# Two half groups of conditioning products summed on VectorE, and the last conditioning products of two groups moved into the norm passages

## The chip, the cores and the metric

The kernel runs on one core of one Trainium2 chip. The number that counts is the device time of one execution in microseconds (us); before the change it is 1595.04 us, the median of 3 runs from 1594.56 to 1595.25 us. The engines are named PE (TensorE, matrix products), DVE (VectorE), ACT (ScalarE), POOL (GpSimd) and SP (the engine that issues the weight loads).

## What is computed

The reference is a transformer of two blocks on 256 tokens of width 1024 (and 256 context tokens in the first layer). What the change touches is the conditioning of the first block:

```python
silu_c, silu_cc = jax.nn.silu(c), jax.nn.silu(c_ctx)
for i in range(2):
    sh1, sc1, g1, sh2, sc2, g2 = split(silu_c @ ada_w[i] + ada_b[i], 6)
    csh1, csc1, cg1, csh2, csc2, cg2 = split(silu_cc @ ada_w[i] + ada_b[i], 6)
    h = rmsnorm(x, norm_mix[i]) * (1.0 + sc1) + sh1      # and hc with csc1, csh1
    x = x + g1 * attention(h, hc)
    h2 = rmsnorm(x, norm_ffn[i]) * (1.0 + sc2) + sh2
    x = x + g2 * conv_ffn(h2)
```

`ada_w[i]` has 1024 rows and 6144 columns. Two vectors (`silu_c`, `silu_cc`) are multiplied with it in layer 0; in layer 1 the context needs only the first third.

## The kernel before

All weights come through one stream, `wstream`, in units of 128 x 2048 numbers (1 MB). `unit_orders` writes the order of the units (`KEYS`) and the order in which PE uses them (`RUNS`). SP loads unit v into buffer v % 3 of `RAW`, and `load_unit` first waits until unit v - 3 has been used up. An ordinary unit is used up when ACT has copied it to its rounded high part (`split_hi`, L526) and DVE or POOL has subtracted to get the low part (`split_lo`, L536), both in `WHL`, which also has three buffers. PE then makes three products for each pair of tiles (L554, L555, L556). Units are split two or three ahead of their use on PE, and every engine takes its instructions strictly in the order in which they are written.

A conditioning unit, key `("ada", b, k)`, is not split. `pe_ada` multiplies it as it stands: `CB` (128 rows, 32 columns, the two vectors in columns 0 and 1) is the stationary operand, the raw unit the moving one, in four products that write the four strips of 32 partitions of one PSUM bank, `AB`. Group b has eight units (four for b = 5 and 6). When a group is complete, ACT copies the bank to `TMP` (`act_ada_row`), PE turns it (`pe_ada_turn`, L599) and DVE adds the bias (`dve_ada`).

Group 1 is spread over the first QKV phase: two units behind each of `("qkv", 0, 3)`, 4 and 5, one behind 6 and 7. Group 3 has two units in the second norm passage, two ahead of up unit 0, and one ahead of each of the up units 2 to 5. Group 4 is made already in another way: DVE multiplies each unit by one vector's column and adds it to `WSUM` (`dve_ada_step`), and `pe_ada_joint` closes the sum over partitions with a column of ones (L586). Of group 5, units 0 to 2 stand in the norm passage ahead of layer 1, and unit 3 behind the first QKV unit; of group 6, units 0 to 2 stand in the norm passage ahead of up unit 0 of layer 1, and unit 3 behind that unit.

In the QKV phase of layer 0, `dve_qkv` does for each unit u: low part of unit u + 3, then the rotation of the two heads of unit u (`stream_shuffle`, a product with the sine table L1106, a sum L1109); the rotation needs a cosine product of POOL (L1121), and POOL makes half of the low parts of every second unit and of all from unit 8.

Of the kernel before, what the change touches and what calls it, by code (L numbers as in the profile page):

```python
# [6 lines left out]
F32 = mybir.dt.float32  # L7
# [142 lines left out]
def unit_orders():  # L150
# [15 lines left out]
    late_ada = iter(range(DT))  # L166
    for i in range(8):
        add(("qkv", 0, i), 1 if i < 3 else 2)
        for _ in range((0, 0, 0, 2, 2, 2, 1, 1)[i]):
            k = next(late_ada)  # L170
            add_ada(1, k)
            run_ada(1, k)
    for i in range(4):
        add(("qkv", 0, 8 + i), 1)
# [8 lines left out]
    for j in range(HALF_FT):  # L183
        add(("up", 0, j), 2)
        for k in {1: range(4), 2: (4,), 3: (5,), 4: (6,), 5: (7,)}.get(j, ()):
            add_ada(3, k)
# [16 lines left out]
    for j in range(FT):  # L203
        add(("up", 1, j), 1000)
        for k in {0: (0, 1, 2), 1: (3,)}.get(j, ()):
            add_ada(6, k)
# [21 lines left out]
    for name, at, b in (("up", UP_ADA, 3), ("qkv", QKV_ADA, 5), ("up", LATE_ADA, 6), ("up", JOINT_ADA, 4)):  # L228
        for key, ks in at.items():
            r = runs.index(key)  # L230
            runs[r:r] = [("ada", b, k) for k in ks]
    return keys, every, runs
# [63 lines left out]


# [67 lines left out]
def bass_two_block_decoder(nc, wstream, first, small, consts, late, rpb, xin, out):  # L365
    ctx = ExitStack()
    with ctx:
# [102 lines left out]
        c_silu, c_zero, lam_v, lam_exp = (sem(n) for n in ("c_silu", "c_zero", "lam_v", "lam_exp"))  # L470
# [88 lines left out]
        def pe_ada(e, b, k):  # L559
            v = UNIT_OF["ada", b, k]  # L560
            if k == 0 and b == 1:
                e.wait_ge(f_par, DT)
            elif k == 0:
                e.wait_ge(ada_par, b - 1)
            e.wait_ge(d_raw[v % 3], 16 * (v // 3 + 1))
            for j in range(4):
                c = k if b < 5 else 2 * k + j // 2
                mm = e.matmul(AB[32 * j:32 * j + 32, :], CB[:, c, :], RAW[:, v % 3, 512 * j:512 * j + 512],  # L568
                              start=k == 0, stop=k == ada_units(b) - 1)
            mm.then_inc(gemm, 1)  # L570

        def dve_ada_step(e, k):
            v = UNIT_OF["ada", 4, k]
            e.wait_ge(d_raw[v % 3], 16 * (v // 3 + 1))
            if k == 0:
                e.tensor_scalar(WSUM[:, :], RAW[:, v % 3, :], CB[:, k, 0:1], None, ALU.mult).then_inc(ada_acc, 1)
                return
            e.wait_ge(ada_acc, k)
            e.scalar_tensor_tensor(out=WSUM[:, :], in0=RAW[:, v % 3, :], scalar=CB[:, k, 0:1], in1=WSUM[:, :],
                                   op0=ALU.mult, op1=ALU.add).then_inc(ada_acc, 1)  # L580
# [469 lines left out]
        def act_qkv(e, l):  # L1050
            for u, i in enumerate(QKV_ORDER[l]):
# [24 lines left out]
                if l == 0 and i == 7:  # L1076
                    act_ada_row(e, 1)
# [3 lines left out]
            for i in range(4):  # L1081
# [402 lines left out]
        def pe_wo(e, l):  # L1484
            T, n = (512, 1) if l == 0 else (256, 3)
            for i in range(4):
# [32 lines left out]
            pe_ada(e, 6 if l else 3, 1)  # L1519
# [69 lines left out]
        def pe_ffn(e, l):  # L1589
            T, ring = (512, 3) if l == 0 else (256, 6)  # L1590
            for c, js in chunks(l):
                for jj, j in enumerate(js):
# [1438 lines left out]
        def act_start(e):  # L3031
# [3 lines left out]
            e.wait_ge(c_zero, 5)  # L3035
# [12 lines left out]
        def dve_start(e):  # L3048
# [6 lines left out]
            e.memset(CB[:, :, :], 0.0).then_inc(c_zero, 1)  # L3055
# [24 lines left out]
        def pool_start(e):  # L3080
            pool_rsqrt(e, 0)
# [288 lines left out]
```

## Time and profile before

| | |
|---|---|
| Median of 3 runs | 1595.04 us |
| The profiled execution | 1595.22 us |
| Its span, first to last instruction | 1593.4 us |
| Mean granted clock of TensorE | 0.997 |
| PE busy | 1568.6 us (98%) |
| DVE busy | 936.4 us (59%) |
| ACT busy | 750.5 us (47%) |
| POOL busy | 543.3 us (34%) |
| Share of PE in the chain that ended last | 88% |

Times in the rows are counted from the start of the span. The busy time of PE is the union of its matmuls, whose ends overlap the start of the next; how long a group of products really takes is therefore read from the starts around it.

### The profile page before, as it was taken

Reading aid. Unit: us, or ns where it says so; the run is one execution under the profiler, and the core shown is the slowest. Engines: PE = TensorE matmul, PEld = TensorE weight load, DVE = VectorE, ACT = ScalarE, POOL = GpSimd, SP = SyncE. Lnnn points to the kernel's source line nnn. Section 1 sums busy time; section 2 is a strip of 40 time slices with the busy share of each in tenths; the row PEclk is TensorE's granted clock in tenths of the full one; section 3 lists DMA queues with packets and bytes.
Section 4 is the critical chain, followed back from the end, with each engine's and each line's share of the span. In section 5 each row is a group of like instructions: output and inputs, shape, how many; then the busy total and the mean of one; then the engine's idle time right before and its main releaser. Section 6 shows DMA issues by size and latency. Waiting matters only on the chain.

```text
span 1593.4 us, 23097 instructions
## 1 busy us (share of the span) xinstructions
PE 1568.6 (98%) x9146; PEld 1303.4 (82%) x9146; DVE 936.4 (59%) x1441; ACT 750.5 (47%) x1360; POOL 543.3 (34%) x354
## 2 busy tenths in 40 slices
PE   8999999999999999999999999999999999999998
PEld 5778557778887888879768899989998889998887
DVE  4434485555575554342266888757876457968435
ACT  5324485444322433243375755445654445654444
POOL 2224243322211222212273111007424657623663
PEclk9999999999999999999999999999999999999999
DMA  9264500534174222364313754454534534633551
GB/s 393 94 246 187 212 30 9 204 135 157 63 268 184 80 81 73 124 207 164 123 37 113 267 192 172 162 190 170 183 133 161 199 143 171 215 133 132 185 211 54
DMA packets 52603, 249.17 MB, mean 156 GB/s; under 512 B 20624, under 2 KB 21008, under 8 KB 26256
## 3 DMA queue, kind: packets, MB, share of 16 engines
q1 hardware_dynamic: 43744, 243.90, 42.2%
q10 hardware_dynamic: 8752, 3.80, 1.0%
q8 instruction: 73, 1.20, 0.3%
q14 instruction: 34, 0.28, 0.0%
HBM read 246.63 MB, written 1.05 MB: 155 GB/s over the span
## 4 chain that ended last, share of the span: by engine, by line
PE 88%; DVE 5%; ACT 3%; issue 1%; DMA 1%; POOL 1%; SPq 0%; POOLq 0%; ACTq 0%; DVEq 0%
PE psq L554 16%; PE psq L555 16%; PE psq L556 16%; PE ps L554 7%; PE ps L556 7%; PE ps L555 7%; PE psq L970 3%; PE ps L568 1%; PE psq L971 1%; PE ps L970 1%; DMA RAW<-wstream 1%; ACT WHL L526 1%; PE psq L1365 1%; PE ps L1393 1%; PE psq L2298 1%
## 5 line engine op out<-in xcount | busy, mean ns | idle before, releaser
L536 DVE TENSOR_TENSOR WHL<-RAW,WHL 128x1024 fp32r<-128x1024 f32 (+3 forms) x264 | 324.9, 1254 | 290.1 <-ACT WHL L526 289.6
L536 POOL TENSOR_TENSOR WHL<-RAW,WHL 128x1024 fp32r<-128x1024 f32 (+2 forms) x116 | 304.5, 2627 | 504.6 <-ACT WHL L526 471.8
L526 ACT ACTIVATE WHL<-RAW 128x1024 fp32r<-128x1024 f32 (+2 forms) x380 | 361.4, 1002 | 196.1 <-DMA RAW<-wstream 98.6
L554 PE MATMUL psq<-NHL,WHL 128*128 128x256 f32 (+1 forms) x1072 | 353.8, 330 | 1.7 <-POOL WHL L536 0.7
L555 PE MATMUL psq<-NHL,WHL 128*128 128x256 f32 (+1 forms) x1072 | 349.0, 326 | 0.0
L556 PE MATMUL psq<-NHL,WHL 128*128 128x256 f32 (+1 forms) x1072 | 348.9, 325 | 0.0
L554 PEld LDWEIGHTS psq<-NHL,WHL 128*128 128x128 f32 x1072 | 205.2, 191 | 28.9 <-issue 7.5
L556 PEld LDWEIGHTS psq<-NHL,WHL 128*128 128x128 f32 x1072 | 205.3, 191 | 16.6
L555 PEld LDWEIGHTS psq<-NHL,WHL 128*128 128x128 f32 x1072 | 205.3, 191 | 15.4
L554 PE MATMUL psq<-WHL,NHL 128*128 128x512 f32 (+1 forms) x320 | 124.8, 390 | 1.7 <-DVE WHL L536 1.7
L556 PE MATMUL psq<-WHL,NHL 128*128 128x512 f32 (+1 forms) x320 | 123.3, 385 | 0.0
L555 PE MATMUL psq<-WHL,NHL 128*128 128x512 f32 (+1 forms) x320 | 123.2, 385 | 0.0
L554 PE MATMUL ps<-NHL,WHL 128*128 128x512 f32 (+1 forms) x272 | 94.9, 349 | 0.0
L555 PE MATMUL ps<-NHL,WHL 128*128 128x512 f32 (+1 forms) x272 | 94.1, 346 | 0.0
L556 PE MATMUL ps<-NHL,WHL 128*128 128x512 f32 (+1 forms) x272 | 94.0, 346 | 0.0
L1716 DVE SCALAR_TENSOR_TENSOR TMP<-psq,SMALL,TMP 128x510 f32<-128x510 f32 (+1 forms) x64 | 39.2, 613 | 79.7 <-ACT TMP L1677 79.7
L699 ACT ACTIVATE TMP<-X 128x256 f32<-128x256 f32 (+1 forms) x52 | 25.1, 498 | 120.7 <-DVE X L1532 59.9
L1677 ACT ACTIVATE TMP<-psq,SMALL 128x512 f32<-128x512 f32 (+1 forms) x64 | 40.8, 666 | 87.0 <-PE psq L556 87.0
L554 PEld LDWEIGHTS psq<-WHL,NHL 128*128 128x128 f32 x320 | 60.1, 188 | 14.3 <-DVE WHL L536 2.1
L556 PEld LDWEIGHTS psq<-WHL,NHL 128*128 128x128 f32 x320 | 60.1, 188 | 11.5
L555 PEld LDWEIGHTS psq<-WHL,NHL 128*128 128x128 f32 x320 | 60.1, 188 | 11.0
L1752 POOL TENSOR_TENSOR HL<-TMP,HH 128x512 fp32r<-128x512 f32 x22 | 28.8, 1308 | 112.9 <-ACT HH L1663 112.9
(389 smaller groups left out, 2975.6 us busy)
## 6 DMA issues: line engine op xcount, KB each, us to landing
RAW<-wstream SPq DMA_DIRECT2D x194, 1024.0 KB, 4.8
RAW<-wstream SPq DMA_DIRECT2D x32, 704.0 KB, 4.0
K<-first SPq DMA_DIRECT2D x4, 1024.0 KB, 17.2
RAW<-wstream SPq DMA_DIRECT2D x4, 800.0 KB, 4.3
X<-xin SPq DMA_DIRECT2D x2, 1024.0 KB, 6.1
V<-first SPq DMA_DIRECT2D x2, 1024.0 KB, 19.3
Q<-first SPq DMA_DIRECT2D x2, 1024.0 KB, 24.7
BR<-rpb ACTq DMA_DIRECT2D x8, 256.0 KB, 8.2
```

The lines of the kernel that those rows point to most:

```text
L526: e.activation(WH[:, u % 3, a:z], RAW[:, v % 3, a:z], ACT.Copy).then_inc(w_hi, 1)
L536: e.tensor_tensor(WL[:, u % 3, a:z], RAW[:, v % 3, a:z], WH[:, u % 3, a:z].bitcast(F32), ALU.subtract).then_inc(w_lo_p if pool else w_lo_v, 1)
L554: e.matmul(o, lh, rh, start=start, stop=False)
L555: e.matmul(o, lh, rl, start=False, stop=False)
L556: return e.matmul(o, ll, rh, start=False, stop=stop)
L568: mm = e.matmul(AB[32 * j:32 * j + 32, :], CB[:, c, :], RAW[:, v % 3, 512 * j:512 * j + 512], start=k == 0, stop=k == ada_units(b) - 1)
L699: e.activation(sq_tile(n, m), X[:, m, 0:NORM_T[n]], ACT.Square).then_inc(x_sq, 1)
L970: e.matmul(o[:, 0:512], wh, x, start=start, stop=False, skip_group_check=True)
L971: return e.matmul(o[:, 0:256], wl, x[:, 0, :], start=False, stop=stop, skip_group_check=True)
L1677: e.activation(acc_tile(l, U, s), up_banks(l, jj)[s][:, :], ACT.Identity, scale=small_at("fconv", (3 * l + 1) * 44 + j + FT * s), bias=sma ...
L1716: e.scalar_tensor_tensor(out=a3[:, :, 1:256], in0=o3[:, :, 0:255], scalar=w(0), in1=a3[:, :, 1:256], op0=ALU.mult, op1=ALU.add).then_inc(u ...
L1752: e.tensor_tensor(HL[l][:, jj, :], acc_tile(l, U, 0), HH[l][:, jj, :].bitcast(F32), ALU.subtract).then_inc(h_lo, 1)
```

## The change

Group 1: units 0, 1, 6 and 7 are multiplied by both vectors and summed on DVE, units 2 to 5 stay on PE in two pairs, and a joint product of the two sums stands behind `("qkv", 0, 8)`. Group 3: units 0 to 3 stay on PE, 4 to 7 are summed on DVE beside the up units 1, 3, 5 and 7, and the joint stands ahead of up unit 8. The sums of group 1 lie in parts of `PP` and `TMP`, those of group 3 in `WSUM`, which is now twice as long. The column of ones is a column of `CB`, and POOL clears `CB` instead of DVE. The fourth unit of the groups 5 and 6 goes into the norm passage ahead of them. The order of the stream follows.

```diff
-UP_ADA = {("up", 0, 0): (0, 1, 2, 3), ("up", 0, 2): (4,), ("up", 0, 3): (5,), ("up", 0, 4): (6,), ("up", 0, 5): (7,)}
-QKV_ADA = {("qkv", 1, 4): (0, 1, 2), ("qkv", 1, 5): (3,)}
-JOINT_ADA = {("up", 0, HALF_FT + 1): (7,)}
-LATE_ADA = {("up", 1, 0): (0, 1, 2), ("up", 1, 1): (3,)}
+FIRST_ADA = {3: (0,), 4: (1,), 5: (2, 3), 6: (4, 5), 9: (6,), 10: (7,)}
+FIRST_SUMMED = {1: (0,), 2: (1,)}
+FIRST_ON_PE = {5: (2, 3), 6: (4, 5)}
+UP_SUMMED = {1: 4, 3: 5, 5: 6, 7: 7}
+QKV_ADA = {("qkv", 1, 4): (0, 1, 2, 3)}
+LATE_ADA = {("up", 1, 0): (0, 1, 2, 3)}
+SUMMED = {1: (0, 1, 6, 7), 3: (4, 5, 6, 7), 4: tuple(range(8))}
+JOINT_AT = {("qkv", 0, 9): 1, ("up", 0, 8): 3, ("up", 0, HALF_FT + 1): 4}
...
         def load_unit(e, v):
...
-            if v >= 3 and KEYS[v - 3][:2] == ("ada", 4):
-                e.wait_ge(ada_acc, KEYS[v - 3][2] + 1)
+            if v >= 3 and KEYS[v - 3] in ADA_ACC:
+                e.wait_ge(ada_acc, ADA_ACC[KEYS[v - 3]])
...
+        def weight_sums(b):
+            if b == 1:
+                return [t.rearrange("p a n -> p (a n)") for t in (PP[:, 3:7, :], TMP[:, 4:8, :])]
+            return [WSUM[:, c, :] for c in range(1 if b == 4 else 2)]
+
+        def dve_ada_step(e, b, k):
+            v = UNIT_OF["ada", b, k]
+            sums = weight_sums(b)
+            at = ADA_ACC["ada", b, k] - len(sums)
             e.wait_ge(d_raw[v % 3], 16 * (v // 3 + 1))
+            if b == 4 and k == 0:
+                e.wait_ge(gemm, product(("joint", 3)))
+            for c, t in enumerate(sums):
+                if k == SUMMED[b][0]:
+                    e.tensor_scalar(t, RAW[:, v % 3, :], CB[:, k, c:c + 1], None, ALU.mult).then_inc(ada_acc, 1)
+                    continue
+                e.wait_ge(ada_acc, at - len(sums) + c + 1)
+                e.scalar_tensor_tensor(out=t, in0=RAW[:, v % 3, :], scalar=CB[:, k, c:c + 1], in1=t,
+                                       op0=ALU.mult, op1=ALU.add).then_inc(ada_acc, 1)
...
+        def pe_ada_joint(e, b):
+            if b == 4:
+                e.wait_ge(ada_par, 3)
+            e.wait_ge(ada_acc, ADA_ACC["ada", b, SUMMED[b][-1]])
+            for c, t in enumerate(weight_sums(b)):
+                for j in range(4):
+                    mm = e.matmul(AB[32 * j:32 * j + 32, :], ONE_AT[c], t[:, 512 * j:512 * j + 512], start=b == 4,
+                                  stop=b == 4 or c == 1)
             mm.then_inc(gemm, 1)
...
             for i in range(4):
                 if l == 0 and i == 1:
+                    pe_ada_joint(e, 1)
+                if l == 0 and i == 2:
                     pe_ada_turn(e, 1)
                 pe_values(e, l, i)
...
         def dve_qkv(e, l):
             for u, i in enumerate(QKV_ORDER[l]):
+                if l == 0:
+                    for k in FIRST_SUMMED.get(i, ()):
+                        dve_ada_step(e, 1, k)
                 split_lo(e, ahead(("qkv", l, i)), False)
...
-            dve_ada(e, 1 if l == 0 else 5)
+            if l == 0:
+                dve_ada_step(e, 1, 6)
+                dve_ada_step(e, 1, 7)
             for i in range(3):
+                if i == (1 if l == 0 else 0):
+                    dve_ada(e, 1 if l == 0 else 5)
                 split_lo(e, ahead(("qkv", l, 8 + i)), False)
...
                 if (l, i) == (1, 3):
                     pe_ada(e, 6, 0)
+                    pe_ada(e, 6, 1)
...
-            pe_ada(e, 6 if l else 3, 1)
+            pe_ada(e, 6 if l else 3, 2 if l else 1)
...
+                        if jj == 8:
+                            pe_ada_joint(e, 3)
...
-                    if l == 1 and j < 2:
-                        pe_ada(e, 6, 2 + j)
+                    if l == 1 and j == 0:
+                        pe_ada(e, 6, 3)
...
+                    if l == 0 and j in UP_SUMMED:
+                        dve_ada_step(e, 3, UP_SUMMED[j])
                     split_lo(e, ahead(key), False)
```

The first place is DVE at the end of the QKV phase of layer 0. WHL is the low part, the K rows are the rotation of the last QKV unit, and ADA is the bias sum that closes group 1. Before:

```order
L536 TENSOR_TENSOR WHL<-RAW,WHL 128x1024
L1104 STREAM_SHUFFLE TMP<-TMP 128x256
L1106 TENSOR_TENSOR TMP<-TMP,CONST 128x256
L1109 TENSOR_TENSOR K<-K,TMP 128x256
L1104 STREAM_SHUFFLE TMP<-TMP 128x256
L1106 TENSOR_TENSOR TMP<-TMP,CONST 128x256
L1109 TENSOR_TENSOR K<-K,TMP 128x256
L619 TENSOR_TENSOR ADA<-ps,SMALL 128x32
L536 TENSOR_TENSOR WHL<-RAW,WHL 128x1024 x3
```

The same place now, where L549 is the low part, L1142 the end of a head's rotation, and L602 a step of the sums:

```order
L549 TENSOR_TENSOR WHL<-RAW,WHL 128x1024
L1137 STREAM_SHUFFLE TMP<-TMP 128x256
L1139 TENSOR_TENSOR TMP<-TMP,CONST 128x256
L1142 TENSOR_TENSOR K<-K,TMP 128x256
L1137 STREAM_SHUFFLE TMP<-TMP 128x256
L1139 TENSOR_TENSOR TMP<-TMP,CONST 128x256
L1142 TENSOR_TENSOR K<-K,TMP 128x256
L602 SCALAR_TENSOR_TENSOR PP<-RAW,CB,PP 128x2048
L602 SCALAR_TENSOR_TENSOR TMP<-RAW,CB,TMP 128x2048
L602 SCALAR_TENSOR_TENSOR PP<-RAW,CB,PP 128x2048
L602 SCALAR_TENSOR_TENSOR TMP<-RAW,CB,TMP 128x2048
L549 TENSOR_TENSOR WHL<-RAW,WHL 128x1024
```

Four steps over 2048 columns stand between the last rotation and the next low part. The second place is PE between `("qkv", 0, 8)` and `("qkv", 0, 9)`. Before, only the turn of group 1 (L599) stands there:

```order
L554 MATMUL psq<-WHL,NHL 128x512
L555 MATMUL psq<-WHL,NHL 128x512
L556 MATMUL psq<-WHL,NHL 128x512
L599 MATMUL ps<-CONST,TMP 128x128 x4
L554 MATMUL psq<-WHL,NHL 128x512
L555 MATMUL psq<-WHL,NHL 128x512
```

Now the joint of group 1 (L614) stands there, and the turn comes one unit later:

```order
L567 MATMUL psq<-WHL,NHL 128x512
L568 MATMUL psq<-WHL,NHL 128x512
L569 MATMUL psq<-WHL,NHL 128x512
L614 MATMUL ps<-PP,CB 32x512 x4
L614 MATMUL ps<-TMP,CB 32x512 x4
L567 MATMUL psq<-WHL,NHL 128x512
L568 MATMUL psq<-WHL,NHL 128x512
```

The joint waits for the last of the four steps on DVE. The third place is PE in the norm passage ahead of layer 1 (L737 sums of squares, L808 the row of scales, L568 conditioning products, L918 and L920 the first QKV unit). Before:

```order
L737 MATMUL ps<-ONES,TMP 128x64 x4
L568 MATMUL ps<-RAW,CB 32x512 x4
L808 MATMUL ps<-CONST,RS 128x128 x4
L568 MATMUL ps<-RAW,CB 32x512 x4
L918 MATMUL psq<-NHL,WHL 128x512
L920 MATMUL psq<-NHL,WHL 128x512
```

And now, with L765, L836, L581, L946 and L948 for the same things:

```order
L765 MATMUL ps<-ONES,TMP 128x64 x4
L581 MATMUL ps<-RAW,CB 32x512 x4
L836 MATMUL ps<-CONST,RS 128x128 x4
L581 MATMUL ps<-RAW,CB 32x512 x8
L946 MATMUL psq<-NHL,WHL 128x512
L948 MATMUL psq<-NHL,WHL 128x512
```

Two conditioning units in place of one stand ahead of the first QKV product.

## Rows read from the trace of the kernel before

**Rows 1.** The page, part 1: PE's busy time, share and instructions.

```profile
PE 1568.6 (98%) x9146; PEld 1303.4 (82%) x9146; DVE 936.4 (59%) x1441; ACT 750.5 (47%) x1360; POOL 543.3 (34%) x354
```

**Rows 2.** Timeline of PE around two units: start, duration, line, shapes.

```profile
75.41 0.39 PE L556 MATMUL psq<-NHL,WHL 128*128 128x512 f32 x1
...
77.93 0.40 PE L555 MATMUL psq<-NHL,WHL 128*128 128x512 f32 x1
...
88.41 0.39 PE L556 MATMUL psq<-NHL,WHL 128*128 128x512 f32 x1
```

**Rows 3.** Timeline of PE around the last single unit of group 1.

```profile
126.52 0.39 PE L556 MATMUL psq<-NHL,WHL 128*128 128x512 f32 x1
...
128.17 0.39 PE L555 MATMUL psq<-WHL,NHL 128*128 128x512 f32 x1
```

**Rows 4.** Instructions on WSUM: count, ns min/median/max, first and last start.

```profile
L579 DVE SCALAR_TENSOR_TENSOR WSUM<-RAW,CB,WSUM x7: 2345/2349/3192, 440.2 to 482.4; 128x2048 f32<-128x2048 f32 x7
L576 DVE TENSOR_SCALAR WSUM<-RAW,CB x1: 1279/1279/1279, 438.9 to 438.9; 128x2048 f32<-128x2048 f32 x1
```

**Rows 5.** Loads into RAW issued between 113 and 117 us, and their landing.

```profile
L511 SPq DMA_DIRECT2D RAW<-wstream x2: 328/352/377, 115.9 to 116.3; - x2
...
DMA to landing us min/median/max: 4.7/5.8/6.8
```

**Rows 6.** Timeline of ACT: the high part of the eighth QKV unit.

```profile
120.57 2.01 ACT L526 ACTIVATE WHL<-RAW 128x1024 fp32r<-128x1024 f32 x2 [7.06 <-DMA RAW<-wstream]
```

**Rows 7.** Timeline of DVE at the end of the QKV phase, layer 0.

```profile
121.67 1.23 DVE L536 TENSOR_TENSOR WHL<-RAW,WHL 128x1024 fp32r<-128x1024 f32 x1 [4.90 <-ACT WHL L526]
...
131.66 0.43 DVE L1104 STREAM_SHUFFLE TMP<-TMP 128x256 f32<-128x256 f32 x1
...
134.22 1.22 DVE L536 TENSOR_TENSOR WHL<-RAW,WHL 128x1024 fp32r<-128x1024 f32 x1
...
135.84 2.13 DVE L1106 TENSOR_TENSOR TMP<-TMP,CONST 128x256 f32<-128x256 f32 x1
...
140.21 0.43 DVE L1109 TENSOR_TENSOR K<-K,TMP 128x256 f32<-128x256 f32 x1
```

**Rows 8.** Timeline of POOL: its halves of two low parts there.

```profile
122.66 2.51 POOL L536 TENSOR_TENSOR WHL<-RAW,WHL 128x1024 fp32r<-128x1024 f32 x1 [7.46 <-ACT WHL L526]
...
134.89 2.80 POOL L536 TENSOR_TENSOR WHL<-RAW,WHL 128x1024 fp32r<-128x1024 f32 x1 [4.25 <-ACT WHL L526]
```

**Rows 9.** Timeline of PE's weight loads near the start.

```profile
3.32 0.34 PEld L742 LDWEIGHTS psq<-PP 128*128 128x128 f32 x1 [0.52 <-issue]
...
10.68 0.30 PEld L742 LDWEIGHTS psq<-PP 128*128 128x128 f32 x2 [0.84 <-issue]
```

**Rows 10.** A stretch: us, then busy PE, PEld, DVE, ACT, POOL; granted clock.

```profile
320.00:420.00 100.00, 100.00 (x455) 79.06 (x454) 57.17 (x61) 43.97 (x59) 24.58 (x15) 1.00 0.37 137
```

**Rows 11.** Timeline of PE in the norm passage ahead of layer 1.

```profile
686.42 1.06 PE L568 MATMUL ps<-RAW,CB 128*32 128x512 f32 x8
688.17 0.47 PE L918 MATMUL psq<-NHL,WHL 128*128 128x512 f32 x1 [0.69 <-ACT NHL L851]
```

**Rows 12.** The load of the group's fourth unit, and its landing.

```profile
L511 SPq DMA_DIRECT2D RAW<-wstream x1: 327/327/327, 683.0 to 683.0; - x1
...
DMA to landing us min/median/max: 4.8/4.8/4.8
```

**Rows 13.** Timeline of PE in the norm passage of layer 1.

```profile
875.78 1.06 PE L568 MATMUL ps<-RAW,CB 128*32 128x512 f32 x8
877.67 1.55 PE L737 MATMUL ps<-ONES,TMP 128*128 128x64 f32 x12 [0.82 <-POOL TMP L719]
...
882.26 0.36 PE L918 MATMUL psq<-NHL,WHL 128*128 128x256 f32 x1 [0.29 <-ACT NHL L851]
```

**Rows 14.** Two loads issued between 874 and 878 us, and their landing.

```profile
L511 SPq DMA_DIRECT2D RAW<-wstream x2: 327/328/328, 874.6 to 876.9; - x2
...
DMA to landing us min/median/max: 4.8/5.0/5.1
```

More of the change, by code:

```diff
@@ L164, in run_ada @@
         runs.append(("ada", b, k))
[L166 to L170, printed above, removed]
+    for i in range(12):
+        add(("qkv", 0, i), 1 if i < 3 or i >= 8 else 2)
+        for k in FIRST_ADA.get(i, ()):
             add_ada(1, k)
+        for k in FIRST_ON_PE.get(i, ()):
             run_ada(1, k)
-    for i in range(4):
-        add(("qkv", 0, 8 + i), 1)
     for i in range(2):
@@ L184, in unit_orders @@
         add(("up", 0, j), 2)
-        for k in {1: range(4), 2: (4,), 3: (5,), 4: (6,), 5: (7,)}.get(j, ()):
+        for k in {1: range(4), 2: (4,), 4: (5,), 6: (6,), 8: (7,)}.get(j, ()):
             add_ada(3, k)
@@ L204, in unit_orders @@
         add(("up", 1, j), 1000)
-        for k in {0: (0, 1, 2), 1: (3,)}.get(j, ()):
+        for k in {0: (0, 1, 2, 3)}.get(j, ()):
             add_ada(6, k)
@@ L227, in unit_orders @@
             add(("out", l, i), 1)
-    for name, at, b in (("up", UP_ADA, 3), ("qkv", QKV_ADA, 5), ("up", LATE_ADA, 6), ("up", JOINT_ADA, 4)):
+    for at, b in ((UP_ADA, 3), (QKV_ADA, 5), (LATE_ADA, 6)):
         for key, ks in at.items():
@@ L231, in unit_orders @@
             runs[r:r] = [("ada", b, k) for k in ks]
+    for key, b in JOINT_AT.items():
+        r = runs.index(key)
+        runs[r:r] = [("joint", b)]
     return keys, every, runs
@@ L295, in product_end @@
     return GEMM_BEFORE[KEYS[v]] + unit_products(KEYS[v])
+ADA_ACC = {}
+acc_count = 0
+for b_, ks_ in SUMMED.items():
+    for k_ in ks_:
+        acc_count += 1 if b_ == 4 else 2
+        ADA_ACC["ada", b_, k_] = acc_count
 SPLIT_UNITS = [v for v, k_ in enumerate(KEYS) if k_[0] != "ada"]
@@ L560, in pe_ada @@
             v = UNIT_OF["ada", b, k]
-            if k == 0 and b == 1:
+            if b == 1 and k == 2:
                 e.wait_ge(f_par, DT)
@@ L568, in pe_ada @@
                 mm = e.matmul(AB[32 * j:32 * j + 32, :], CB[:, c, :], RAW[:, v % 3, 512 * j:512 * j + 512],
-                              start=k == 0, stop=k == ada_units(b) - 1)
+                              start=k == (2 if b == 1 else 0), stop=k == ada_units(b) - 1)
             mm.then_inc(gemm, 1)
-        def dve_ada_step(e, k):
-            v = UNIT_OF["ada", 4, k]
-            e.wait_ge(d_raw[v % 3], 16 * (v // 3 + 1))
[L575 to L580, printed above, removed]
@@ L588, in pe_ada_joint @@
             mm.then_inc(gemm, 1)
         def act_ada_row(e, b):
-            e.wait_ge(gemm, product(("ada", b, ada_units(b) - 1)))
+            e.wait_ge(gemm, product(("joint", b) if b in SUMMED else ("ada", b, ada_units(b) - 1)))
             if b >= 2:
@@ L1000, in pe_qkv @@
             n = 2 * l
-            late_ada = iter(range(DT))
             for u, i in enumerate(QKV_ORDER[l]):
@@ L1022, in pe_qkv @@
                 if l == 0:
-                    for _ in range((0, 0, 0, 2, 2, 2, 1, 1)[i]):
-                        pe_ada(e, 1, next(late_ada))
+                    for k in FIRST_ON_PE.get(i, ()):
+                        pe_ada(e, 1, k)
             for i in range(4):
                 if l == 0 and i == 1:
+                    pe_ada_joint(e, 1)
+                if l == 0 and i == 2:
                     pe_ada_turn(e, 1)
@@ L1599, in pe_ffn @@
                     if l == 0 and c == 0:
-                        for k in UP_ADA.get(("up", 0, jj), ()):
-                            if k > 1:
-                                pe_ada(e, 3, k)
+                        if jj == 0:
+                            pe_ada(e, 3, 2)
+                            pe_ada(e, 3, 3)
+                        if jj == 8:
+                            pe_ada_joint(e, 3)
                         if jj == 9:
```

29 lines of the change are left out of this document (15 added, 14 removed).

## The prediction

> **What bounds the kernel now.** I read the page's engine shares first. The reader is to see that PE is busy for 1568.6 of 1593.4 us and DVE for 936.4 [rows 1]: PE is the bound, and a microsecond taken from PE or added to it in a dense stretch moves the end by as much. Then the timeline of PE, for what one conditioning group really takes; then the DVE, ACT, POOL and load rows around 120 to 141 us, since the change makes PE wait there for DVE; last the two norm passages.
>
> In a QKV unit a product of 512 columns follows the one before at (88.41 - 77.93) / 46 = 0.228 us [rows 2]. With a pair of conditioning units between, L555 comes 2.52 us after the last L556, where two steps would be 0.46: a pair costs 2.06 us [rows 2]. A single unit costs 128.17 - 126.52 - 0.46 = 1.19 us [rows 3].
>
> **Group 1, the products.** Before: three pairs and two singles, 3 x 2.06 + 2 x 1.19 = 8.56 us. Now two pairs and the joint, which has the shape and count of a pair: 6.18. That is **-2.4 us** on PE.
>
> **Group 1, the new wait.** The joint waits for DVE's steps 6 and 7. When does PE arrive? At 128.17 it starts the second product of QKV unit 8 with 8.56 us of groups behind it; now only two pairs, 4.12, are behind it, so it is there at 123.73, and 47 more steps of 0.228 bring it to the joint at 134.4.
>
> When is DVE done? The load of QKV unit 8 is issued behind a conditioning product: at 115.9, landing after 4.7 [rows 5], and ACT starts on it at 120.57 [rows 6]. In the new order it waits for the first product of the pair behind QKV unit 6, which comes two pairs (4.1 us) earlier; so ACT starts at 116.5 and DVE's low part at 117.6 in place of 121.67 [rows 7]. From 121.67 to the last sum of the rotation at 140.21 + 0.43 = 140.64 DVE works almost without a gap [rows 7], so the change's earlier loads bring it forward by 4.1 us, to 136.5. The load of QKV unit 10 is no longer late: its buffer comes free with POOL's half, at 122.66 + 2.51 - 4.1 = 121.1 [rows 8], so it lands at 125.9 and POOL's half of it (2.80 us [rows 8]) starts near 128. POOL's work then lies beside the rotation of unit 6 in place of that of unit 7. A rotation of two heads takes 134.22 - 131.66 = 2.6 us alone, and 5.2 (140.64 less 135.44) with POOL's half beside it, one table product of 2.13 us among it [rows 7]; it hits one or the other, so the end stays about 136.5. Behind it come four steps of 2.35 us [rows 4], 9.4 in all: step 7 ends at 145.9. Queued behind them are the low part of QKV unit 11, which PE needs two units later, and the bias sum, which now waits for a later turn; neither holds anybody.
>
> So PE waits 145.9 - 134.4 = 11.5 us. Bounds: if POOL disturbed nothing, the low part of unit 10 is done one half high part and 1.2 us after 125.9, near 128.1, the rotation at 130.7 and the steps at 140.1: 5.7 us. With all four steps at the slowest row, 3.19 us [rows 4], it is 14.9. I take **+11.0 us**, near the sum from the rows, since the disturbed rotation is what the trace shows. There is nothing behind the joint that PE could do first; its queue is in order. ACT takes the row out of the bank behind the joint, and the turn comes a unit later, hidden.
>
> **The clock after the wait.** No stretch of the trace shows a wait of PE this long in the middle; the granted clock is 1.00 in the up phase [rows 10]. At the start of the span, after PE had done nothing, a weight load of 128 columns takes 0.34 us at 3.32 and 0.15 at 10.68 (two in 0.30) [rows 9]: the lower of its two levels, 1.2 GHz, and then the upper, 2.4. The level rose somewhere between, so 3.3 to 10.7 us at the low level would lose half of that, 1.6 to 5.3 us. Whether 11 us of waiting brings it down, the rows can't say; below it is nothing. I take **+2.0 us**, near the smaller price.
> The Trainium skill, "TensorE: Matmul & The Clock Gate", Part 1 (The HAM clock gate), says that an idle PE falls back to half rate and gets the full rate back only after working for a while. By that rule the term is certain and not only likely; the start of this trace agrees with the second half of it, and the first is not shown. Without the rule the sum would be 2 us lower.
>
> **Group 3.** Four singles (4.76 us) become one joint pair (2.06): **-2.7 us**. DVE gets 2 x 1.28 + 6 x 2.35 = 16.7 us more [rows 4] over eight up units. It is busy 57 of 100 us there while PE has no gap [rows 10], a unit is split two ahead and PE's next use of a bank is three units off, so a step of 4.7 us in every second unit is covered by 43 us of idle DVE. If that cover failed, one late step would cost up to 4.7. Step 7 ends in the middle of up unit 7, before the joint. The joint of group 4 is as it was.
>
> **The norm passages.** Each loses a single group behind the first unit, -1.19. In the passage ahead of layer 1 the third product starts at 686.42 and ends by 687.4; the load of the fourth unit was issued at 683.0 and lands after 4.8, at 687.8 [rows 12]; the fourth product then runs to 688.9, where the first QKV product starts now at 688.17 after a wait of 0.69 for ACT [rows 11]. So +0.7 and -1.2: **-0.5**. In layer 1 the second product goes into the 0.82 us that PE waits for POOL before the sums at 877.67 [rows 13], 875.78 + 2 = 877.8, no loss. The third and fourth units are the loads of 874.6 and 876.9, landing after 4.8 to 5.1 [rows 14], the last at 881.9; its product ends at 882.9, against 882.26 for the first up product now [rows 13]. Again +0.7 - 1.2: **-0.5**. Bounds for the two together: -2.4, if nothing were late, to +1.0, if the scales came late as well.
>
> **The rest.** CB cleared by POOL instead of DVE: the first products at the start wait for the sums of squares and for loads, not for it; 0. Loads of group 1 that now wait for DVE's steps 0 and 1 (2.6 and 4.7 us, some 10 us ahead of PE's need): 0.
>
> **Sum.** -2.4 + 11.0 + 2.0 - 2.7 - 0.5 - 0.5 = +6.9. Against the profiled execution's own 1595.22 us (span 1593.4 and 1.8 around it) this is 1602.1; that execution lies 0.2 above the median of the runs, so I say 1602 us. All that the change removes, 6.1 us, is less than the one wait that it makes.
>
> **Rivals.**
> 1. *DVE is nearly in time (the faster side).* If the joint waits less than 3 us and the clock stays, the time is 1589.1 (no wait) to 1592. For it: DVE is busy only 59% overall [rows 1]. Against: four steps of 2.35 us can't start before the rotation of unit 7, whose last input PE delivers itself only 11 us before it arrives at the joint, and 9.4 us of these are the steps. It decides where wait and clock together fall below 6.1 us. Chance 0.11.
> 2. *A shorter wait, warm.* The wait is 5.7 to 9 us, as POOL disturbs less, and the clock holds: 1595 to 1598. For it: the lower bound above. Chance 0.16.
> 3. *The clock comes back late.* The price of the clock is 5.3 instead of 2.0, or the wait 14: 1605 to 1608. Chance 0.08.
> 4. *DVE is late in the up phase too.* One step of 4.7 us uncovered: 1607. Against it the 43% of idle DVE [rows 10]. Chance 0.03.
> The forecast (wait 9 to 13, clock 0 to 3) has 0.62, and its own range is 1598 to 1605.
>
> **Chances and range.** This kernel can be told from no change by about 0.2%, 3.2 us. The forecast but for a sliver (0.03), rivals 3 and 4 and a small part of the second (0.03) are slower by more: 0.73. Within 0.2% are the most of the second and that sliver: 0.16. Faster: the first rival, 0.11. The range 1595.5 to 1606 leaves out the first rival and the far end of the third.
>
> **What would show it.** Right: in the profile after, PE has one gap of about 11 us before the joint of group 1 near 134 us, released by DVE's step on TMP, and the steps are four of 2.35 us in a row behind the rotation; weight loads just behind it at 0.34 us if the clock fell; no gap at the joint of group 3; the first products behind the two passages 0.7 us later and the group behind the first unit gone. Wrong: the last step of group 1 ends before PE is done with QKV unit 8, or the loads of that phase come later than I have them, so that PE waits elsewhere first.

## The result, and the profile after

The changed kernel takes 1603.43 us (median of 4 runs, 1603.0 to 1604.47) against 1595.04 us before: a ratio of 1.0054, 95% interval 1.0037 to 1.0071. It is slower by 8.4 us, where 1602 was predicted. Its profiled execution took 1603.0 us, with a span of 1601.2 against 1593.4.

First the line of the page that answers to [rows 1]:

```profile
PE 1564.5 (98%) x9114; PEld 1302.8 (81%) x9114; DVE 969.8 (61%) x1456; ACT 749.3 (47%) x1360; POOL 542.4 (34%) x356
```

PE is busy 4.1 us less, and the span is 7.8 us longer. So what is new is mostly time in which PE does nothing. The waits of PE (whole span; engine, operand and line, what released it: us in total, times, longest) name it at the top of the list:

```profile
PE ps L614 <- DVE TMP L602: 11.1, 1, 11.1
...
PE psq L567 <- DVE WHL L549: 2.4, 3, 0.8
PE ps L581 <- DMA RAW<-wstream: 2.3, 4, 1.1
```

L614 is the joint's product, L602 the step of a weighted sum on VectorE. The timeline of PE at the joint of group 1, and behind it the first products of QKV unit 9:

```profile
146.54 1.93 PE L614 MATMUL ps<-PP,CB 128*32 128x512 f32 x8 [11.12 <-DVE TMP L602]
148.25 1.93 PE L614 MATMUL ps<-TMP,CB 128*32 128x512 f32 x8
150.11 0.80 PE L567 MATMUL psq<-WHL,NHL 128*128 128x512 f32 x1
150.70 0.63 PE L568 MATMUL psq<-WHL,NHL 128*128 128x512 f32 x1
151.13 0.46 PE L569 MATMUL psq<-WHL,NHL 128*128 128x512 f32 x1
151.43 0.40 PE L567 MATMUL psq<-WHL,NHL 128*128 128x512 f32 x1
```

One gap of 11.12 us. Then the joint takes 150.11 - 146.54 = 3.57 us, and a QKV product 0.6 to 0.8 us in place of 0.4: the clock fell. The granted clock by stretches (columns as in [rows 10]; the granted clock is the number behind POOL's) shows the two levels, 2.4 GHz as 1.00 and 1.2 GHz as 0.50:

```profile
118.50:146.50 28.00, 16.92 (x75) 13.48 (x73) 26.58 (x31) 8.35 (x18) 11.94 (x9) 0.84 0.45 166
...
130.00:135.00 5.00, 5.00 (x23) 4.14 (x23) 4.90 (x9) 0.00 (x0) 2.95 (x3) 1.00 0.49 192
135.00:138.00 3.00, 0.42 (x2) 0.00 (x0) 2.86 (x8) 0.00 (x0) 0.00 (x0) 0.93 0.00 0
138.00:150.50 12.50, 3.96 (x17) 0.98 (x18) 9.71 (x5) 2.26 (x3) 1.35 (x1) 0.50 0.59 223
151.00:152.00 1.00, 1.00 (x5) 0.77 (x5) 0.00 (x0) 0.00 (x0) 0.60 (x1) 0.87 0.36 139
```

The reader is to see VectorE in them as well: busy for 26.58 of the 28 us up to the joint (the first row), and for 2.86 of 3 where PE begins to idle. It is no idle engine that PE waits for. Its timeline, with the three slow table products of the rotations, the last sum of the rotation, and the first and the last of the four steps:

```profile
120.62 1.80 DVE L1139 TENSOR_TENSOR TMP<-TMP,CONST 128x256 f32<-128x256 f32 x1
...
124.20 2.15 DVE L1139 TENSOR_TENSOR TMP<-TMP,CONST 128x256 f32<-128x256 f32 x1
...
129.12 2.56 DVE L1139 TENSOR_TENSOR TMP<-TMP,CONST 128x256 f32<-128x256 f32 x1
...
137.01 0.42 DVE L1142 TENSOR_TENSOR K<-K,TMP 128x256 f32<-128x256 f32 x1
137.35 2.34 DVE L602 SCALAR_TENSOR_TENSOR PP<-RAW,CB,PP 128x2048 f32<-128x2048 f32 x1
...
144.14 2.34 DVE L602 SCALAR_TENSOR_TENSOR TMP<-RAW,CB,TMP 128x2048 f32<-128x2048 f32 x1
```

How far the changed kernel stands behind the one before, by the same row of PE in both traces (starts in us; the last column is a second profiled execution of the changed kernel, out of the experiments):

| place | before | changed | difference | changed, second execution |
|---|---|---|---|---|
| last selection product of the start | 55.24 | 55.92 | +0.68 | -0.06 |
| first unit of group 2, behind the gap | 177.18 | 189.09 | +11.91 | +11.34 |
| joint of group 4, behind group 3 | 507.82 | 516.85 | +9.03 | +8.59 |
| first unit of group 5 (passage ahead of layer 1) | 681.88 | 690.92 | +9.04 | +8.59 |
| turn of group 5 | 750.74 | 758.76 | +8.02 | +7.60 |
| first unit of group 6 (passage in layer 1) | 875.78 | 883.80 | +8.02 | +7.61 |
| turn of group 6 | 918.69 | 926.85 | +8.16 | +7.79 |
| span | 1593.4 | 1601.2 | +7.8 | +7.8 |

### The profile page after: what moved, and what is told of

It is laid out like the page before. It is cut to its first block, busy times and chain, and to the rows that moved or that the text cites. A ratio compares the mean times of both kernels' runs of the same rounds, so it can differ in the third digit from the quotient of the medians.

```text
span 1601.2 us, 23057 instructions
## 1 busy us (share of the span) xinstructions
PE 1564.5 (98%) x9114; PEld 1302.8 (81%) x9114; DVE 969.8 (61%) x1456; ACT 749.3 (47%) x1360; POOL 542.4 (34%) x356
## 4 chain that ended last, share of the span: by engine, by line
PE 81%; DVE 10%; ACT 4%; issue 2%; DMA 2%; POOL 1%; ACTq 0%; POOLq 0%; SPq 0%; DVEq 0%
PE psq L567 14%; PE psq L569 14%; PE psq L568 14%; PE ps L567 7%; PE ps L569 7%; PE ps L568 7%; PE psq L998 3%; DVE WHL L549 2%; ACT WHL L539 2%; PE psq L999 1%; PE ps L998 1%; DMA RAW<-wstream 1%; PE psq L1402 1%; PE ps L1430 1%; PE ps L1417 1%
## 5 line engine op out<-in xcount | busy, mean ns | idle before, releaser
L549 DVE TENSOR_TENSOR WHL<-RAW,WHL 128x1024 fp32r<-128x1024 f32 (+3 forms) x264 | 329.6, 1272 | 257.8 <-ACT WHL L539 257.3
L549 POOL TENSOR_TENSOR WHL<-RAW,WHL 128x1024 fp32r<-128x1024 f32 (+2 forms) x116 | 302.5, 2610 | 496.5 <-ACT WHL L539 463.8
L568 PE MATMUL psq<-NHL,WHL 128*128 128x256 f32 (+1 forms) x1072 | 348.2, 325 | 0.0
L568 PEld LDWEIGHTS psq<-NHL,WHL 128*128 128x128 f32 x1072 | 204.6, 191 | 15.6
L568 PE MATMUL psq<-WHL,NHL 128*128 128x512 f32 (+1 forms) x320 | 123.4, 386 | 0.0
L568 PE MATMUL ps<-NHL,WHL 128*128 128x512 f32 (+1 forms) x272 | 94.1, 346 | 0.0
L568 PEld LDWEIGHTS psq<-WHL,NHL 128*128 128x128 f32 x320 | 60.3, 188 | 11.0
```

What stands on the lines that cost most here:

```text
L549: e.tensor_tensor(WL[:, u % 3, a:z], RAW[:, v % 3, a:z], WH[:, u % 3, a:z].bitcast(F32), ALU.subtract).then_inc(w_lo_p if pool else w_lo_v, 1)
L568: e.matmul(o, lh, rl, start=False, stop=False)
```

## The experiments

Eight kernels were run, in two batches; all but the repeat are edits of the changed kernel. An edit is shown as the lines that say it; comments stand for the rest. Ratios are against the kernel before, run beside them on the same chip (medians 1595.62 and 1595.13 us), with the 95% interval.

### The joint one unit and a quarter later

```
-JOINT_AT = {("qkv", 0, 9): 1, ...
+JOINT_AT = {("qkv", 0, 10): 1, ...
 # pe_values, per quarter t of a unit
+    if l == 0 and i == 2 and t == 1:
+        pe_ada_joint(e, 1)
+    if l == 0 and i == 2 and t == 2:
+        pe_ada_turn(e, 1)
 # act_qkv: act_ada_row(e, 1) between the evictions t = 1 and t = 2 of unit 9
```

> The joint of group 1 stands one unit of V and a quarter later (behind the first quarter of unit 10, its turn behind the second, the copy of its row in the midst of the evictions of V's first half); nothing else differs from the changed kernel. PE would then come to the joint at about 135.4 + 10.5 + 2.6 = 148.5 us, 2 us after the last step (146.5). Theory A (the wait of 11.1 us is all that is wrong, and the slow clock behind it is its consequence): no wait at the joint, no granted clock of 0.50 from 138 to 151, attention and all behind it earlier by 11.1 + 2.3 = 13.4 us: 1603.4 - 13.4 = 1590.0, under the kernel before. Theory B (PE at the joint only waits in place of something later: the split of unit 11, whose load also hangs on the steps and whose high part ran at 147.1 in the changed kernel): some of it comes back as a wait for unit 11's low part or at the first scores, 1593 to 1600. Theory C (the clock falls here whether or not PE waits): 1592.3.

Measured: 1589.93 us (5 runs, 1589.46 to 1592.26), ratio 0.9965 (0.9952 to 0.9979). PE's joint has no wait in the timeline, and the stretch in which PE idled is full at a granted clock of 1.00:

```profile
148.31 1.06 PE L614 MATMUL ps<-PP,CB 128*32 128x512 f32 x8
149.19 1.04 PE L614 MATMUL ps<-TMP,CB 128*32 128x512 f32 x8
```

```profile
138.00:142.00 4.00, 4.00 (x19) 3.32 (x18) 4.00 (x3) 0.00 (x0) 0.00 (x0) 1.00 0.02 6
142.00:147.00 5.00, 5.00 (x24) 4.14 (x23) 4.34 (x2) 0.28 (x1) 0.00 (x0) 1.00 0.81 305
```

VectorE does the same steps at the same time (the first at 137.21, the last until 146.35 us); only PE's order differs. The first unit of group 2 starts at 175.06, 2.12 us ahead of the kernel before. Theory A holds and B falls: nothing else was waiting behind the joint. C falls too, by the clock of 1.00. This kernel is faster than the changed one by 13.5 us and faster than the one before by 0.35%.

### The joint directly ahead of unit 10

The edit is against the late joint:

```
-    if l == 0 and i == 2 and t == 1:
+    if l == 0 and i == 2 and t == 0:
         pe_ada_joint(e, 1)
```

> The joint of group 1 directly ahead of unit 10's first quarter, 2.6 us earlier than in late_joint; its turn and all else as there. PE arrives at about 145.0, the last step ends at about 146.3. Theory A (the wait is arrival against the last step, and a short wait leaves the clock at 1.00): wait of 1.3 us, joint in 1.9 us, granted clock 1.00, total 1589.93 + 1.3 = 1591.2. Theory B (any wait here costs the clock): 1591.2 + 2.3 = 1593.5. Theory C (arrival and steps move together, as both hang on the same rotations): a wait well under 1 us, 1590.

Measured: 1590.68 us (9 runs, 1589.4 to 1593.7), ratio 0.9974 (0.9964 to 0.9984).

```profile
146.51 1.07 PE L614 MATMUL ps<-PP,CB 128*32 128x512 f32 x8 [0.86 <-DVE TMP L602]
147.39 1.04 PE L614 MATMUL ps<-TMP,CB 128*32 128x512 f32 x8
```

```profile
142.00:147.00 5.00, 4.14 (x25) 2.88 (x27) 4.46 (x2) 0.23 (x1) 0.00 (x0) 1.00 0.79 288
```

The wait is PE's arrival against the last step, which again ends near 146.5. PE came at 146.51 - 0.86 = 145.65, 0.65 later than the expectation has it, so the wait is shorter than theory A's 1.3. A wait of 0.86 us left the clock at 1.00: B falls. The median lies about midway between A's 1591.2 and C's 1590 and can't tell these two apart; that the steps end where they did in the changed kernel speaks for A. In time the two late joints can't be told apart either.

### Two of the four steps cut short

```
 for c, t in enumerate(sums):
+    if b == 1 and k >= 6 and c == 1:
+        e.tensor_scalar(JUNK[:, 2 * k:2 * k + 2], RAW[:, v % 3, 0:2], CB[:, k, c:c + 1], None, ALU.mult)...
+        continue
```

> The second vector's sum leaves out units 6 and 7 of group 1: two of the four long steps on VectorE (2.34 us each) become steps of two columns (0.06 us). The last step then ends at about 137.35 + 2 x 2.34 + 0.1 = 142.2 in place of 146.5. Theory A (VectorE's last step sets the joint, one for one, and the clock's loss is a fixed amount as long as the wait is long enough for it to fall): the wait is 6.8 us in place of 11.1, clock still 0.50 behind it, 1603.4 - 4.4 = 1599.0. Theory B (the clock's loss grows with the wait): 1599.0 less up to 1.0, 1598.0. Theory C (PE really waits for a load or the split of unit 11, not the steps): 1603.4.

Measured: 1599.31 us (11 runs, 1598.34 to 1602.25), ratio 1.0023 (1.0015 to 1.0032), 0.3 from theory A. PE's timeline, and the clock by stretches:

```profile
142.02 1.94 PE L617 MATMUL ps<-PP,CB 128*32 128x512 f32 x8 [7.54 <-DVE JUNK L599]
```

```profile
134.00:138.00 4.00, 0.47 (x3) 0.05 (x1) 3.86 (x10) 0.00 (x0) 0.00 (x0) 0.86 0.00 0
138.00:142.00 4.00, 0.00 (x0) 0.00 (x0) 3.96 (x4) 0.00 (x0) 0.00 (x0) 0.50 0.38 96
142.00:147.00 5.00, 4.98 (x19) 1.76 (x20) 0.78 (x1) 1.87 (x2) 0.00 (x0) 0.50 0.98 411
```

The steps end 4.5 us earlier (142.0 against 146.5) and so does the joint. Here PE came to it at 142.02 - 7.54 = 134.48, so the wait is 7.5 and not 6.8. The clock falls all the same: from the joint's start to the first unit of group 2 it takes 184.75 - 142.02 = 42.73 us, against 42.55 in the changed kernel. C falls, and B too: 7.5 us of waiting cost the clock as much as 11.1.

### Products that fill the gap

```
 if l == 0 and i == 1:
+    for _ in range(12):
+        pe_constant(e, bank[4], 512)
     pe_ada_joint(e, 1)
```

> Twelve products of zeros with zeros (128x128 by 512 columns, fp32, into a bank that nobody reads then) stand ahead of the joint of group 1; at 5.6 us for eight passes at the start of the span (0.7 to 0.85 us each) they take 9 to 10.2 us of the 11.1 that PE waits. Theory A (the granted clock falls because PE is idle): the clock stays at 1.00, the joint takes 1.9 us in place of 3.6, and the whole is shorter by the 2.3 us that the clock cost: 1603.4 - 2.3 = 1601.1, with a wait of 1 to 2 us left at the joint. Theory B (the 2.3 us are not the clock's, or the filling products delay VectorE through the shared steps before them): 1603.4 or more.

The tile they read, FILL, holds ones and not zeros as the expectation has it; nobody reads what they write either way.

Measured: 1601.9 us (5 runs, 1600.11 to 1603.95), ratio 1.0038 (1.0025 to 1.005).

```profile
135.83 10.46 PE L770 MATMUL ps<-PP 128*128 128x512 f32 x24
147.59 1.06 PE L614 MATMUL ps<-PP,CB 128*32 128x512 f32 x8 [1.30 <-DVE TMP L602]
148.47 1.04 PE L614 MATMUL ps<-TMP,CB 128*32 128x512 f32 x8
```

```profile
138.00:142.00 4.00, 4.00 (x11) 1.85 (x10) 3.96 (x4) 0.00 (x0) 0.00 (x0) 1.00 0.00 0
142.00:147.00 5.00, 4.29 (x10) 1.55 (x9) 5.00 (x3) 0.00 (x0) 0.00 (x0) 1.00 0.57 203
```

The same delay, but PE works through it and the clock stays at 1.00. From the joint's start to the first unit of group 2 it now takes 187.93 - 147.59 = 40.34 us. The same work, from the end of QKV unit 8 to group 2, takes 175.06 - (134.39 + 0.39) = 40.28 us with the late joint, so this base is no accident of one trace. That is the clean price of the clock: 42.55 - 40.34 = 2.2 us in the changed kernel, 42.05 - 40.34 = 1.7 in its second execution (joint at 146.47, group 2 at 188.52), 42.73 - 40.34 = 2.4 with the short steps. From the joint's start until the clock was back at 1.00 (151.2, 150.0 and 147.1 us) PE worked 4.7, 3.5 and 5.1 us at 0.50, and half of each, 2.3, 1.8 and 2.6, is the price within 0.2 us: what it costs is set by how long PE works slowly behind the wait, and not by the wait's length.

The median is lower than the changed kernel's, but the runs scatter by 3.8 us, so here the trace and not the median carries the reading. The scatter goes with the clock elsewhere: the fastest run, 1600.11 us, has a mean granted clock of 1.000, and the profiled one, the slowest, 0.996, with 0.50 near 15, 892 and 1394 us.

### Group 1 on PE again, the rest as changed

```
-FIRST_ADA = {3: (0,), 4: (1,), 5: (2, 3), 6: (4, 5), 9: (6,), 10: (7,)}
-FIRST_SUMMED = {1: (0,), 2: (1,)}
-FIRST_ON_PE = {5: (2, 3), 6: (4, 5)}
+FIRST_ADA = {3: (0, 1), 4: (2, 3), 5: (4, 5), 6: (6,), 7: (7,)}
+FIRST_SUMMED = {}
+FIRST_ON_PE = FIRST_ADA
 # turn ahead of unit 9; no steps 6 and 7 in dve_qkv
```

> Group 1 of the conditioning is again all on PE in its old order (eight units inside Q and K, no steps on VectorE, turn ahead of unit 9); group 3's sums, the order in both norm passages and the clearing of CB on GpSimd stay as changed. Theory A (the rest of the change is worth what the landmarks of the changed kernel's trace show: +0.7 at the start of the span, -2.76 in group 3, -1.0 and +0.1 in the two passages, -0.4 later): 1595.0 - 3.4 = 1591.7, or 1591.0 without the +0.7 at the start. Theory B (most of those are drift between two profiled executions and only the products that go are worth something): 1595.0 - 2.7 = 1592.3 at best, 1594 if the passages give nothing and the start costs 0.7 and more.

Measured: 1593.52 us (11 runs, 1591.83 to 1594.39), ratio 0.9983 (0.9974 to 0.9992). Against the kernel before, its trace stands at +0.06 at the first unit of group 2 (177.24), -2.44 at the joint of group 4 (505.38; -2.80 from the start of group 3 at +0.36), -3.34 at the turn of group 5, -3.22 at the turn of group 6, and -2.4 at the end. So the terms of theory A are in the trace, but the median is 1.8 us above it, at the far end of what B allows. The single runs lie in two clusters, 1591.8 to 1592.2 and 1593.5 to 1594.4; the kernel before, run beside it, has two as well, 1594.8 to 1595.3 and 1596.4 to 1596.7, so a difference of medians also compares how many runs fell into each. Lower against lower it is about 3.0 us, upper against upper about 2.8, by medians 2.1. Of the 3.2 us that this trace has gained at 918 us, 0.8 is lost again behind it, where no edit reaches; where that goes was not settled.

### Group 6 in its old order

On top of the late joint:

```
-LATE_ADA = {("up", 1, 0): (0, 1, 2, 3)}
+LATE_ADA = {("up", 1, 0): (0, 1, 2), ("up", 1, 1): (3,)}
 # pe_wo: unit 1 behind the sums; pe_up: units 2 and 3 behind up units 0 and 1
```

> As late_joint (the joint of group 1 behind the first quarter of unit 10), and group 6 of the conditioning in the norm passage of layer 1 in its old order again: its second unit behind the sums, its last one behind the up group's second unit. In late_joint the passage of layer 1 made the kernel 0.74 us longer (start of its pair at -5.94 us against the kernel before, turn of group 6 at -5.20), with waits of 0.82 and 0.88 us for the loads of the third and the fourth unit. Theory A (the added loads between the norm and the second up unit push that up unit's low part): the turn of group 6 stands at the same -5.94 as the start of the passage, total 1589.93 - 0.7 = 1589.2. Theory B (the loads were late whatever the order; the same 0.7 is waited for elsewhere): 1589.9.

Measured: 1589.76 us (5 runs, 1588.77 to 1590.88), ratio 0.9964 (0.9952 to 0.9977). In time it is not to be told from the late joint alone. In the trace it is: the first unit of group 6 starts at 869.66 (-6.12), the turn at 912.54 (-6.15), so the passage costs nothing again. PE's rows in that passage, first with the late joint alone (the changed order), then with the old order:

```profile
874.11 1.06 PE L581 MATMUL ps<-RAW,CB 128*32 128x512 f32 x8 [0.82 <-DMA RAW<-wstream]
...
876.69 1.06 PE L581 MATMUL ps<-RAW,CB 128*32 128x512 f32 x8 [0.88 <-DMA RAW<-wstream]
...
884.60 0.38 PE L567 MATMUL psq<-NHL,WHL 128*128 128x256 f32 x1 [0.89 <-DVE WHL L549]
```

```profile
871.54 1.55 PE L765 MATMUL ps<-ONES,TMP 128*128 128x64 f32 x12 [0.82 <-POOL TMP L747]
873.03 1.06 PE L581 MATMUL ps<-RAW,CB 128*32 128x512 f32 x8
```

The changed order fills the 0.82 us before the sums, but then waits for both loads and, in the next up unit, for VectorE's low part. By the trace this is theory A; the medians, 0.2 us apart, can't show it. The edit puts back both the place of the second unit and that of the fourth, so it does not say which of them costs; the rows in the next section do.

### CB cleared on VectorE, and the changed kernel once more

```
 # dve_start, behind the squares (and no longer in pool_start)
+e.memset(CB[:, :, :], 0.0).then_inc(cb_zero, 1)
+e.wait_ge(cb_zero, 1)
+e.memset(CB[:, 0, 16:17], 1.0).then_inc(cb_zero, 1)
```

> As best, and CB is cleared (and given its column of ones) on VectorE behind the squares, as in the kernel before, in place of GpSimd at the start. In two of five executions of kernels with the clearing on GpSimd, the clock fell to 0.50 from 15 to 18 us and the start phase ended 0.7 and 1.1 us later; in three it did not, nor in the kernel before. Theory A (chance: the start is on the edge whoever clears CB): as best, 1589.2, within 0.5 us, and the spread of the single runs (about 1.5 us between a lower and an upper cluster) is the same. Theory B (the clearing on GpSimd and the earlier table load on ScalarE cause it): all single runs in the lower cluster and no 0.50 in the profile.

> The changed kernel once more, beside the others on the same chip. If the slow clock at 15 to 18 us is chance, some of its executions are without it: single runs between 1602.3 (without) and 1603.9 (with), the arrival at the joint at 134.5 in an execution without it (135.4 in the one with it), and a wait at the joint of 12.0 - 0 us less whatever VectorE gains by the earlier start; if it belongs to the kernel, 0.50 stands there again and all runs are at 1603 and above.

Measured: 1590.01 us (6 runs, 1589.17 to 1591.67), ratio 0.9968 (0.9956 to 0.9979), and for the repeat 1603.64 us (5 runs, 1602.38 to 1604.25), ratio 1.005 (1.0038 to 1.0063). The start of the span by stretches, first with CB cleared on VectorE, then the changed kernel the second time:

```profile
15.00:16.00 1.00, 1.00 (x7) 1.00 (x6) 1.00 (x2) 1.00 (x2) 0.00 (x0) 0.50 1.04 434
16.00:17.00 1.00, 1.00 (x4) 0.36 (x2) 1.00 (x3) 0.17 (x2) 0.00 (x0) 0.50 0.99 418
```

```profile
15.00:16.00 1.00, 1.00 (x9) 0.75 (x7) 1.00 (x2) 1.00 (x2) 0.00 (x0) 1.00 1.02 426
16.00:17.00 1.00, 0.95 (x10) 0.34 (x12) 1.00 (x3) 0.20 (x2) 0.00 (x0) 1.00 0.97 410
```

Here the slow clock at 15 to 18 us comes with the old clearing and is absent with the new one, and the changed kernel has it in one execution and not in the other. So it goes with neither: theory A. Three of the ten profiled executions have it (the changed kernel's first, the filled gap, and this one), and their start phase ends 0.7 to 1.1 us later. The second execution of the changed kernel is without it and has the same span, 1601.2: its wait at the joint was 11.61 us.

## Why the prediction was right, step by step

- **Group 1's products.** Predicted -2.4, measured -2.1: the late joint, with neither wait nor slow clock, starts group 2 2.12 us earlier.
- **Group 1's wait.** Predicted 11.5 by the sum and 11.0 taken, measured 11.12 and 11.61. PE arrives at 135.42 (134.86 the second time) in place of 134.4, of which 0.7 is the slow start. The last step ends at 146.5 in place of 145.9, since VectorE's chain came forward by 3.0 us and not by 4.1. It begins with ScalarE's high part of QKV unit 8, taken at 116.5 and measured in both executions at 117.55:

```profile
117.55 2.01 ACT L539 ACTIVATE WHL<-RAW 128x1024 fp32r<-128x1024 f32 x2 [4.46 <-DMA RAW<-wstream]
```

Its load, issued at 112.5 (111.7 the second time), landed after 5.1 us (5.8) and not after 4.7. The chain itself is as long as before: 18.8 us from the low part of unit 8 at 118.64 to the end of the rotation at 137.43, against 19.0 [rows 7]. The prediction names one slow table product; the trace before has three (1.80, 2.13 and 2.13 us), and so has this one (1.80, 2.15, 2.56): the third moved from unit 7 to unit 6 as forecast, and the rotation of unit 7 is undisturbed. The steps are the four of 2.34 us. PE and VectorE were both later than forecast, by 1.0 and 0.6 us in one execution and by 0.5 and 0.6 in the other; that the difference held is in part luck.
- **The clock.** Predicted +2.0, between 0 and 5.3; measured +2.2 (+1.7 the second time). The weight loads that were to show it are there: 0.34 us at 150.27 against 0.19 at 151.90. (The 0.15 of the prediction is two overlapping loads halved.) The bounds came from the start of the span and were wide; that the smaller price was nearly right was a guess. The Trainium skill, "TensorE: Matmul & The Clock Gate", Part 1 (The HAM clock gate), says that an idle PE falls back to half rate: these traces agree, with 0.50 behind waits of 11.1 and 7.5 us and 1.00 behind one of 0.86.
- **Group 3.** Predicted -2.7, measured -2.76 (and -2.80 and -2.77 in two experiments). No gap at its joint, which starts at 408.86: the idle VectorE there covered the steps.
- **Passage ahead of layer 1.** Predicted -0.5, measured -1.0 in all traces. The four units and the first QKV product there:

```profile
695.46 1.06 PE L581 MATMUL ps<-RAW,CB 128*32 128x512 f32 x8
696.84 1.06 PE L581 MATMUL ps<-RAW,CB 128*32 128x512 f32 x8 [0.32 <-DMA RAW<-wstream]
697.84 0.50 PE L946 MATMUL psq<-NHL,WHL 128*128 128x512 f32 x1
```

The first QKV product starts 2.38 us behind the third unit, against 688.17 - 686.42 = 1.75 before [rows 11]: 0.6 later, as forecast, and the single unit behind the first QKV unit is gone (1.0). Not forecast: the unit's own products, now behind the norm's last parts, run through in 11.1 us in place of 11.5. Some 0.2 more is between there and the turn.
- **Passage in layer 1.** Predicted -0.5, measured +0.1 to +0.7 in six traces with this order, and +1.9 in the seventh. This is the step that failed. The prediction counts the group that goes from behind up unit 0 as -1.2. But PE could not have begun up unit 1 earlier: before, the group filled just the time in which VectorE made that unit's low part.

```profile
888.48 2.36 DVE L536 TENSOR_TENSOR WHL<-RAW,WHL 128x1024 fp32r<-128x1024 f32 x2 [1.34 <-ACT WHL L526]
```

```profile
888.81 1.07 PE L568 MATMUL ps<-RAW,CB 128*32 128x512 f32 x8
889.81 0.39 PE L554 MATMUL psq<-NHL,WHL 128*128 128x256 f32 x1
```

The first of the two halves is done near 889.7, and the group at 889.81. Now, without the group, PE waits there instead:

```profile
896.67 2.36 DVE L549 TENSOR_TENSOR WHL<-RAW,WHL 128x1024 fp32r<-128x1024 f32 x2 [1.35 <-ACT WHL L539]
```

```profile
896.61 0.64 PE L952 MATMUL psq<-NHL,WHL 128*128 128x256 f32 x4
897.95 0.39 PE L567 MATMUL psq<-NHL,WHL 128*128 128x256 f32 x1 [0.71 <-DVE WHL L549]
```

The low part comes behind the norm's last work on ScalarE and VectorE, and that behind PE's row of scales (L836), which now stands behind the third unit. The third unit waits 0.2 to 0.8 us for its load, and the row of scales, the low part and the turn of group 6, counted from the start of the passage, all move by that against before: by 0.18, 0.17 and 0.14 us in the changed kernel, by 0.78, 0.78 and 0.74 with the late joint. So the fourth unit's place gains nothing, and the third unit's wait, put at nothing, is the whole cost. It is not the load of up unit 1, issued behind the fourth unit's: that landed at 892.7, and ScalarE took it up at 895.60 without a wait for it. The seventh trace, the filled gap, waited 2.19 us for the fourth unit's load, and had the clock at 0.50 from 892 to 895 behind it. With the old order the passage costs nothing, as shown.
- **CB on POOL, loads behind steps 0 and 1.** Predicted 0, and nothing in the traces against it; the start's +0.7 is the chance slow clock.

Together: -2.1 + 11.1 + 2.2 - 2.8 - 1.0 + 0.1 = +7.5, +0.7 at the start and -0.4 behind the turn of group 6, is the +7.8 of the spans. Of the -0.4, some 0.3 is the clock again: between 1370 and 1400 us the kernel before has a mean granted clock of 0.94 and the changed one 1.00. The forecast was +6.9. Rival 1 (VectorE in time) and rival 2 (a wait of 5.7 to 9 us, warm) fell by the wait itself, 11.1 and 11.6 us, and rival 2 by the clock as well, which fell behind 7.5 us of wait too. What the change removes from PE is real, and comes out once PE is not made to wait for it: two experiments end at 1589.8 and 1589.9 us, 5 us below the kernel before.

## What to carry to other kernels

Work that is moved from the bound engine to an idle one pays only if the point where the results meet lies behind the helper's last step; compute that step's end from the rows of the helper around that point, not from its share of the whole span. Here the helper was idle for 39% of the span and for 5% of the 28 us that counted; the meeting point, moved from 134.9 to 148.3 us past work that PE had to do anyway, turned +0.5% into -0.35%. Before work is taken out of a place in the bound engine's order, ask what ends beside it: here a group of 1 us stood where PE would have waited for VectorE anyhow, and taking it away gained nothing.

## What the runs showed of the chip

- A wait of PE of 7.5 us costs as much clock as one of 11 (2.4 and 1.7 to 2.2 us), one of 0.86 us costs none. In the changed kernel the granted clock was 0.50 from 138 to 151 us; PE had last worked at 135.4, and worked again from 146.5. In its second execution it was 0.50 from 140 to 150.
- Products of ones with ones, whose result nobody reads, kept the clock at 1.00 through 10.46 us and behind them.
- At the start of the span, where from 1.5 us on PE's waits are no longer than 0.8 us, the clock fell to 0.50 for 3 us in three of ten executions and not in the others, whatever the kernel: a difference of 1 us between two executions that no edit explains.
- It fell so in the middle of dense work as well, with PE at 0.94 to 1.00 busy: for 3 us between 1124 and 1138 us in four of the ten executions and between 1379 and 1394 in seven, the kernel before among both. The first cost nothing that shows. Behind the second, from the eight 16-column products that stand just ahead of it (1381.47 us before, 1389.58 now) to the end of the span, six of the seven took 211.9 us and one 212.4, the three without it 211.6 to 211.7: 0.2 to 0.3 us, though PE worked for 3 us at half the clock.
- Loads of 1 MB at the same place of the program landed after 4.8 to 5.4 us (third unit of group 6), 5.1 to 6.5 (fourth) and 6.9 to 8.2 (up unit 1) in the seven executions with the changed order; the margin of a transfer is not one number.
